# Expert weights loaded as one 16 KB run a partition, with the columns of h and of act permuted by strided VectorE reads

## The reference

```
x = x + mixer(rms_norm(x, attn_norm))
h = rms_norm(x, ffn_norm)                 # x * rstd * norm weight, 512 x 1024
x = x + hierarchical_moe(h)
...
for e in range(16):
    act = silu(h @ w_gate[e]) * (h @ w_up[e])          # w_gate, w_up: 1024 x 512
    y = y + combine[:, e:e + 1] * (act @ w_down[e])    # w_down: 512 x 1024
```

## Time and profile before

| | |
|---|---|
| median of 3 runs | 1287.82 us (1285.38 to 1289.57) |
| the profiled execution | 1285.25 us, span 1283.5 us |
| PE busy | 1180.3 us (92%) |
| DVE busy | 914.7 us (71%) |
| ACT busy | 674.1 us (53%) |
| DMA, all queues | 281.75 MB, mean 220 GB/s |
| expert stages | about 360 to 660 us and 965 to 1265 us of the span |

### The profile page before, as it was taken

One profiled execution on the slowest core, in us unless ns is written; L12 is line 12 of the kernel. 1 busy time (PEld: TensorE's weight loads), 2 busy tenths in 40 slices (PEclk: granted clock), 3 DMA queues, 4 the chain that ended last, 5 costly groups with the idle time before them and its releaser, 6 DMA issues.

```text
span 1283.5 us, 16959 instructions
## 1 busy us (share of the span) xinstructions
PE 1180.3 (92%) x5788; PEld 898.5 (70%) x5788; DVE 914.7 (71%) x1251; ACT 674.1 (53%) x843; POOL 97.3 (8%) x128
## 2 busy tenths in 40 slices
PE   5999879999799999999878999999979999999986
PEld 4776669878776766766646688887876666667663
DVE  4646668656579888888967247646558898888886
ACT  4335651134347778777733242132426777787862
POOL 1120000000010000000030000001001100000003
PEclk9999999999899999999989999999979999999998
DMA  6231110123599999999860240113169999999955
GB/s 221 91 89 66 66 66 1 66 73 125 187 331 363 366 385 390 384 382 384 332 220 1 70 136 15 66 66 131 66 257 303 368 381 381 383 391 385 381 203 209
DMA packets 129423, 281.75 MB, mean 220 GB/s; under 512 B 18945, under 2 KB 19457, under 8 KB 129361
## 3 DMA queue, kind: packets, MB, share of 16 engines
q1 hardware_dynamic: 119680, 246.98, 53.2%
q0 software_dynamic: 5888, 20.97, 5.3%
q10 hardware_dynamic: 3792, 12.98, 2.7%
HBM read 262.05 MB, written 18.87 MB: 219 GB/s over the span
## 4 chain that ended last, share of the span: by engine, by line
PE 57%; DVE 25%; issue 9%; ACT 6%; POOL 1%; DMA 1%; DVEq 1%; ACTq 0%; SPq 0%
PE PS L1109 16%; PE PS L1111 15%; PE PS L1110 15%; DVE expert_w_low L1824 10%; PE PS L1213 4%; DVE group_low L1612 2%; PE PS L1343 2%; ACT weight_high L870 1%; PE PS L1148 1%; DVE xgT_low L1832 1%; DVE act L1845 1%; DVE score_max L1743 1%; DVE G L1502 1%; PE PS L1323 1%; DVE hT_low L1596 1%
## 5 line engine op out<-in xcount | busy, mean ns | idle before, releaser
L1824 DVE TENSOR_TENSOR expert_w_low<-expert_w,weight_high 128x1024 fp32r<-128x1024 f32 x368 | 426.5, 1221 | 75.0 <-ACT weight_high L870 71.3
L870 ACT ACTIVATE weight_high<-expert_w 128x1024 fp32r<-128x1024 f32 x384 | 375.5, 1049 | 69.6 <-PE PS L1111 61.9
L1109 PE MATMUL PS<-weight_high,xgT_high 128*96 128x512 f32 x512 | 204.5, 399 | 2.6 <-DVEq L1834 2.6
L1111 PE MATMUL PS<-weight_high,xgT_low 128*96 128x512 f32 x512 | 203.2, 397 | 0.0
L1110 PE MATMUL PS<-expert_w_low,xgT_high 128*96 128x512 f32 x512 | 202.1, 395 | 0.0
L1109 PE MATMUL PS<-group_high,hT_high 128*128 128x512 f32 x416 | 172.2, 414 | 13.9 <-DVEq L1599 9.5
L1111 PE MATMUL PS<-group_high,hT_low 128*128 128x512 f32 x416 | 165.3, 397 | 0.0
L1110 PE MATMUL PS<-group_low,hT_high 128*128 128x512 f32 x416 | 165.0, 397 | 0.0
L1109 PE MATMUL PS<-weight_high,actT_high 128*96 128x512 f32 x256 | 104.3, 407 | 19.4 <-DVEq L1882 18.9
L1612 DVE TENSOR_TENSOR group_low<-group_w,group_high 128x1024 fp32r<-128x1024 f32 x68 | 80.8, 1223 | 43.4 <-ACT group_high L894 39.5
L1109 PEld LDWEIGHTS PS<-weight_high,xgT_high 128*96 128x96 f32 x512 | 83.3, 163 | 36.0 <-DVEq L1834 2.7
(11 more groups left out here) (251 smaller groups left out, 1469.9 us busy)
## 6 DMA issues: line engine op xcount, KB each, us to landing
expert_w<-in_moe_w_gate SPq DMA_DIRECT2D x32, 2048.0 KB, 13.7
expert_w<-in_moe_w_up SPq DMA_DIRECT2D x32, 2048.0 KB, 15.0
expert_w<-in_moe_w_down SPq DMA_DIRECT2D x32, 2048.0 KB, 13.5
group_w<-in_even_w_in SPq DMA_DIRECT2D x6, 2048.0 KB, 7.8
group_w<-in_odd_w_in SPq DMA_DIRECT2D x6, 2048.0 KB, 8.1
y_rows<-yb ACTq DMA_DIRECT2D x30, 384.0 KB, 6.1
group_w<-in_even_w_out SPq DMA_DIRECT2D x2, 2048.0 KB, 7.9
h_rows<-h SPq DMA_DIRECT2D x8, 512.0 KB, 11.3
```

Source lines behind the costliest of these rows:

```text
L870: act_(hi, w, ACT.Copy).then_inc(w_hi, 1)
L1109: pe.matmul(out, ah, bh, start=first, stop=False)
L1111: return pe.matmul(out, al, bh, start=False, stop=final)
L1824: tt(lo, w, hi.bitcast(F32), ALU.subtract).then_inc(w_lo, 1)
```

## The change

It has three parts that belong together. The load of an expert weight gives partition p the 8 (or 4) rows that follow each other in memory, so piece k holds rows p*8+k (or p*4+k). VectorE's h of the two expert stages (n = 1 and 3; the mixers' h, n = 0 and 2, stays) is written in the matching order: it reads x and the norm weight with a stride of 8 elements (32 bytes) and writes h without gaps. VectorE's act reads up (PSUM) and `ex` (SBUF) with a stride of 4 elements (16 bytes) and writes act without gaps. The gathered rows, the stored `h_rows` and the transposes then carry the new order by themselves; the router reads x, not h.

```diff
-                    src = t["moe_w_" + name][l, bass.ds(e, 1)].rearrange("a (k p) n -> p (a k) n", p=P)
+                    src = t["moe_w_" + name][l, bass.ds(e, 1)].rearrange("a (p k) n -> p (a k) n", p=P)
...
+            act_parts = act[0:CAP].rearrange("p (k j) -> p k j", k=DE // P)
+
+            def in_parts_of(a):
+                return a.rearrange("p (j k) -> p k j", k=DE // P)
...
-                        stt(h[:, i], x[:, i], xrs[:, i:i + 1], normw[:], ALU.mult, ALU.mult).then_inc(h_ready, 1)
+                        dst, xi, nw = h[:, i], x[:, i], normw[:]
+                        if n % 2:
+
+                            dst = dst.rearrange("p (k j) -> p k j", k=KD)
+                            xi, nw = (a.rearrange("p (j k) -> p k j", k=KD) for a in (xi, nw))
+                        stt(dst, xi, xrs[:, i:i + 1], nw, ALU.mult, ALU.mult).then_inc(h_ready, 1)
...
-                    link(tt(act[0:CAP], bank(("up", l))[0:CAP], ex[0:CAP], ALU.mult))
+                    link(tt(act_parts, in_parts_of(bank(("up", l))[0:CAP]), in_parts_of(ex[0:CAP]), ALU.mult))
...
-                        tt(act[0:CAP], PS[0:CAP, 1, :], ex[0:CAP], ALU.mult).then_inc(ov_ve[l], 1)
+                        tt(act_parts, in_parts_of(PS[0:CAP, 1, :]), in_parts_of(ex[0:CAP]), ALU.mult).then_inc(ov_ve[l], 1)
```

## The result

| | before | after |
|---|---|---|
| median of the first runs | 1287.82 us (1285.38 to 1289.57, 3 runs) | 1301.55 us (1297.39 to 1303.14, 3 runs) |
| ratio | | 1.0102, 95% interval 1.0056 to 1.0147 |
| the same two kernels again | 1286.97 us (12 runs) | 1296.79 us (1291.66 to 1302.03, 6 runs) |
| ratio | | 1.0079, 95% interval 1.0053 to 1.0104 |
| profiled execution: time, span, granted clock | 1285.25, 1283.5, 0.968 | 1301.55, 1299.7, 0.965 |

The change makes the kernel slower by 0.8 to 1.0%, 10 to 14 us. The forecast was 1299 us, slower.

The account below looks back on a forecast made before the run. PE sets the pace with DVE right behind, and DMA keeps up. Per layer 0.74 (h) + 3.7 + 1.1 (acts) = 5.5 us, 11.1 for two, on 1287.82 gives 1299 us; own range 1295 to 1303, wider range 1287 to 1313.

Parts of the forecast that it names:

- Loads at 0: Expert loop: longer runs likely make loads 5 to 10% faster, worth 0, since nothing waits for a load.
- 0.72 ns an element: VectorE's strided reads: price taken from one 16-byte-stride line, adding 0.37 us to act and 0.74 us to h.
- rival 2: VectorE's act and h: strides are free in these two-level patterns, 1288 us, no change; chance 0.18.
- Ten acts a layer in full: Acts of the odd experts, 0 and 14: nothing covers their growth, 10 x 0.37 = 3.7 us a layer.
- Six even acts at 0.18: Acts of even experts 2 to 12: ACT's first part covers 0.19 us, leaving 6 x 0.18 = 1.1 us a layer.
- PE has no slack in front of down: Down in both kinds of expert: DVE's low parts release PE, so uncovered time added to act is added to PE's.
- h at 0.74 a layer: Fourth h tile, before the routing: its 0.74 us joins a chain where PE only waits; second and third are covered.
- The back edge: Loop end, experts 5, 7, 9, 11: the branch waits for act, ACT's part ended 0.4 us earlier; nothing covers act.
- the marks: Expected signs: PE's `actT_low` waits up some 9 us from 18.9, 0.95 at back edges, two-expert round longer by 0.55 us.

Follow-up runs that it names:

- unlinked kernels: Kernel before and changed kernel, each with VectorE not waiting for its own act to complete: 1288.69 us, ratio 1.0016, and 1288.03 us, 1.0011.
- the change again: The changed kernel run again without further edits, against the kernel before: 1296.79 us, ratio 1.0079.

## Why the prediction was right

- **Loads at 0.** Right: 1.001 with loads alone. The landing of the gates went from 13.7 to 11.8 us, and nothing waited for them in either kernel. What the forecast left out is the gather ahead of the loop: it looked for such waits in the loop only, and the changed kernel has one of 0.84 to 1.36 us in layer 0.
- **0.72 ns an element.** Right in size: act +0.39 us for 0.37 forecast, h +0.80 to 1.0 for 0.74. The row of four strided elements at a time priced patterns of 128 elements in a row, so rival 2 fell. Which input pays was left open, and is settled: the one in SBUF. The note of the Trainium skill (SBUF — State Buffer, below "Door 1: The DMA port swizzle") is borne out in its two hits a line (8 bytes free, 16 not) and contradicted in its 4 fp32 for free, by 1077 ns for ex. Its PSUM lines of 8 bytes, which it ties to slower matmuls, cost VectorE nothing when it reads up at 16 bytes (681 ns).
- **Ten acts a layer in full.** Right: nine steps between acts grow by 0.38 to 0.44 us in each layer, and the tenth, act 15, has its followers outside the table: down starts 3.09 and 3.08 us behind it for 2.73, +0.36. 10 x 0.39 = 3.9 for 3.7.
- **Six even acts at 0.18.** Wrong as a term of the sum in layer 0, and two thirds right in layer 1. They cost next to 0 in layer 0 (18.13 to 18.14; 0.07 for act 2) and 0.13 in layer 1 (18.13 to 18.26), 0.1 and 0.7 us in all for 1.1 each. The delay is there: down starts 6.68 us behind act for 6.41, and PE waits 0.24. But the step "PE has no slack in front of down" took PE's delay for the round's. DVE's next wait behind `actT_low` shrinks from 1.55 us (first row below) to 1.27 (573.69 above), and the next act comes when DVE is through with the low parts of gate. These start behind `xgT_low` and behind ACT's first high part of gate, and that one starts when PE is done with the place. Here are ACT and DVE at the gate weight, in layer 0 before, layer 0 after, layer 1 before and layer 1 after:

```profile
529.98 4.63 DVE L1824 TENSOR_TENSOR expert_w_low<-expert_w,weight_high 128x1024 fp32r<-128x1024 f32 x4 [1.55 <-ACT weight_high L870]
...
534.43 3.91 ACT L870 ACTIVATE weight_high<-expert_w 128x1024 fp32r<-128x1024 f32 x4 [0.95 <-PE PS L1111]
535.80 4.63 DVE L1824 TENSOR_TENSOR expert_w_low<-expert_w,weight_high 128x1024 fp32r<-128x1024 f32 x4 [0.32 <-ACT weight_high L870]
```
```profile
578.43 3.91 ACT L870 ACTIVATE weight_high<-expert_w 128x1024 fp32r<-128x1024 f32 x4 [1.23 <-PE PS L1111]
579.52 4.63 DVE L1834 TENSOR_TENSOR expert_w_low<-expert_w,weight_high 128x1024 fp32r<-128x1024 f32 x4 [0.33 <-ACT weight_high L870]
```
```profile
1138.77 3.91 ACT L870 ACTIVATE weight_high<-expert_w 128x1024 fp32r<-128x1024 f32 x4 [1.02 <-PE PS L1111]
1140.05 4.64 DVE L1824 TENSOR_TENSOR expert_w_low<-expert_w,weight_high 128x1024 fp32r<-128x1024 f32 x4 [0.32 <-ACT weight_high L870]
```
```profile
1189.41 3.90 ACT L870 ACTIVATE weight_high<-expert_w 128x1024 fp32r<-128x1024 f32 x4 [1.34 <-PE PS L1111]
1190.50 4.63 DVE L1834 TENSOR_TENSOR expert_w_low<-expert_w,weight_high 128x1024 fp32r<-128x1024 f32 x4 [0.45 <-ACT weight_high L870]
```

  Counted from the even act, ACT starts 0.28 us later in layer 0 (12.22 to 12.50) and DVE's low parts don't (13.59 in both): there were 0.3 us of slack, and PE's delay just fits. In layer 1 ACT started 0.08 later to begin with, and PE waits 0.36 where it waits 0.24 in layer 0. ACT goes from 12.30 to 12.62, and the low parts from 13.58 to 13.71: the 0.13. That is read from these rows; no run changed this slack alone.
- **h at 0.74 a layer.** Right for the start of the routing (+0.8 us in layer 0) and for PE's wait at L1333 (+0.75 a layer in the changed kernel), but too large as a term of the time. The forecast carried the delay on undiminished; some 0.3 us of it come out of the next product in layer 0, and 0.3 stand at act 0 where the clock was the same. The run with h alone can't tell 1.5 us from nothing.
- **The back edge.** The forecast said that nothing covers act there because the branch waits for it and ACT's first part had ended 0.4 us before the low parts start. The pair of unlinked kernels shows both: without the wait the low parts start 1.14 us behind the start of act in place of 1.44, and ACT's part starts 0.1 later there. Whether the branch or the plain wait in front of it binds was not separated: the edit takes act out of both.

The acts account for 3.62 + 4.29 us in the experts and 2 x 0.36 for act 15, **8.6 us** for 9.6 forecast. From h's last tile to act 0 of layer 0 the two traces of the changed kernel take 37.33 and 36.79 us for 36.85: h's delay, the wait for the gather and the higher clock together come to +0.5 and -0.1 us, where the forecast had 0.74. With 0.3 us a layer for h the sum is 9.2 us for 11.1 forecast, beside 9.2 to 10.4 measured for the reads alone and the change again, whose intervals reach down to 7.8 and 6.8 us. The forecast of 1299 was near to the first median (1301.55) partly by chance: with three runs and a granted clock that moves the span by some 5 us, that median came out high, and the traced execution of it was 4.5 us late before the change could act. Of the marks, PE's waits for `actT_low` rose by 7.5 us for 9, the back edges show 0.69 (layer 0) and 0.73 (layer 1) for 0.95, and the round grew by 0.40 us in layer 0 (36.32 to 36.72) and by 0.52 in layer 1 (36.37 to 36.89) for 0.55, all three for the reason of the even acts.

## What to carry to other kernels

Price a layout change on the side that has no slack. Here the loads had 7 us to spare and gained nothing, while 0.39 us on one VectorE instruction of each expert stood in the recurring path in every second expert, and partly in the others. If rows must be matched by strides, put the stride on the PSUM input or keep it at 8 bytes, or free the engine from waiting for its own completed instruction at a loop's back edge, and the same stride is hidden in the loop. (Here both inputs of act carry the same columns, so to leave ex in order ScalarE would have to write it permuted; no run tried what that costs.) And in a loop where two engines are nearly level, add delays along the cycle that closes the round, not in front of every instruction that is seen to wait, and look for the slack of each engine that hands them on.

## What the runs showed of the hardware

- VectorE, fp32, 96 x 512, two inputs: a stride of 16 bytes on the SBUF input costs 0.77 ns an element (681 to 1077 ns); on the PSUM input 0 (681); 8 bytes on both 0 (679). With a stride of 32 bytes on its two SBUF inputs h (128 x 1024) costs 0.8 to 1.0 ns an element (1284 ns in order, 2080 to 2290 ns strided).
- TensorE's fp32 weight load of 96 x 128: 140 ns in order, 209 at 16 bytes, 202 at 32.
- Splitting one VectorE instruction of 512 columns into four of 128 costs 0.19 us in all; each is recorded with 278 ns, and they overlap.
- Runs of 16 KB in place of 2 and 4 KB cut the loads' packets from 119,680 to 50,048 and their queue's share by 3 points, and delayed the short transfers beside them: gathers 7.2 to 10.8 us, stores 6.1 to 8.3 us (11.0 and 8.4 with the loads alone).
